# VectorE's work at three stage boundaries of a two-block network is cut into pieces and reordered

## The reference, cut to what matters

```python
# end of block 1: feed-forward, 5632 hidden columns, then gate and residual
ffn = (silu(h2 @ w_ffn_gate) * (h2 @ w_ffn_up)) @ w_ffn_down
x = x + gate2 * ffn
# block 2, layer 0: the context and the tokens are normed, modulated and projected
h_ctx = layer_norm(ctx) * (1 + sc_c) + sh_c
h_lat = layer_norm(x) * (1 + sc_l) + sh_l
z_ctx = h_ctx @ w_in_attn        # only the columns of keys and values
z_lat = h_lat @ w_in_attn
# block 2, layer 1: 4096 columns u and 4096 columns gate
u, gate = split(h @ w_in_fourier, 2)
f = fft2(u.reshape(b, l, 16, 256), axes=(1, 3), norm="ortho").real
x = post_norm(x, (f * silu(gate)) @ w_out_fourier, ...)
```

## Time and profile before

| | |
|---|---|
| three runs | 2520.95, 2525.25, 2533.34 us |
| profiled execution | 2525.53 us, span of the trace 2523.7 us |
| TensorE matmul busy | 2404.8 us, 95% of the span |
| VectorE busy | 1651.3 us, 65% |
| ScalarE busy | 1047.6 us, 42% |
| GpSimd busy | 220.7 us, 9% |
| DMA | 589.44 MB, mean 234 GB/s |
| mean granted TensorE clock | 0.981 |

### The profile page before, as it was taken

One profiled execution on the slowest core, in us unless ns is written; L12 is line 12 of the kernel. 1 busy time (PEld: TensorE's weight loads), 2 busy tenths in 40 slices (PEclk: granted clock), 3 DMA queues, 4 the chain that ended last, 5 costly groups with the idle time before them and its releaser, 6 DMA issues.

```text
span 2523.7 us, 37893 instructions
## 1 busy us (share of the span) xinstructions
PE 2404.8 (95%) x15430; PEld 2058.3 (82%) x15430; DVE 1651.3 (65%) x1869; ACT 1047.6 (42%) x1386; POOL 220.7 (9%) x200
## 2 busy tenths in 40 slices
PE   5899989989999999999999999999978999999996
PEld 1588765569888899888887888888768999999995
DVE  8655645456888888886677566555664585765557
ACT  2354764224333333333343454444443343334332
POOL 0139700011000000000011100000012000000000
PEclk9899999999999999999999999999999999999998
DMA  9844469968999999997553754334445675675451
GB/s 386 321 156 153 156 257 372 402 221 297 356 357 350 358 379 354 347 348 272 155 185 116 227 170 129 103 103 134 168 133 176 217 263 173 231 243 178 152 191 57
DMA packets 257582, 589.44 MB, mean 234 GB/s; under 512 B 20608, under 2 KB 29824, under 8 KB 256128
## 3 DMA queue, kind: packets, MB, share of 16 engines
q1 hardware_dynamic: 257408, 587.02, 67.0%
HBM read 584.85 MB, written 2.10 MB: 233 GB/s over the span
## 4 chain that ended last, share of the span: by engine, by line
PE 88%; DVE 5%; DMA 3%; ACT 2%; issue 1%; POOL 1%; SPq 0%; DVEq 0%; ACTq 0%
PE psum L213 13%; PE psum L225 13%; PE psum L227 12%; PE psum L226 12%; PE psum L215 12%; PE psum L214 12%; PE psum L297 3%; DMA start_slots<-in_w_ada 2%; DVE wlo L202 1%; PE psum L1905 1%; PE psum L2526 1%; PE psum L487 1%; PE psum L755 1%; PE psum L1919 1%; PE psum L882 1%
## 5 line engine op out<-in xcount | busy, mean ns | idle before, releaser
L202 DVE TENSOR_TENSOR wlo<-raw,whi 128x1024 fp32r<-128x1024 f32 (+2 forms) x728 | 879.6, 1224 | 558.3 <-ACT whi L196 554.9
L196 ACT CAST whi<-raw 128x1024 fp32r<-128x1024 f32 (+2 forms) x728 | 740.1, 1026 | 938.1 <-PE psum L227 491.7
L225 PE MATMUL psum<-hh,whi 128*128 128x256 f32 x2688 | 759.9, 283 | 4.9 <-DVE wlo L202 4.4
L226 PE MATMUL psum<-hh,wlo 128*128 128x256 f32 x2688 | 750.8, 279 | 0.0
L227 PE MATMUL psum<-hl,whi 128*128 128x256 f32 x2688 | 750.7, 279 | 0.0
L225 PEld LDWEIGHTS psum<-hh,whi 128*128 128x128 f32 x2688 | 507.5, 189 | 21.9 <-DVE wlo L202 11.7
L227 PEld LDWEIGHTS psum<-hl,whi 128*128 128x128 f32 x2688 | 511.5, 190 | 0.0
L226 PEld LDWEIGHTS psum<-hh,wlo 128*128 128x128 f32 x2688 | 507.8, 189 | 1.8 <-issue 1.0
L213 PE MATMUL psum<-whi,hh 128*128 128x512 f32 (+1 forms) x720 | 292.6, 406 | 9.6 <-DVE wlo L202 6.2
L215 PE MATMUL psum<-whi,hl 128*128 128x512 f32 (+1 forms) x720 | 282.3, 392 | 0.0
L214 PE MATMUL psum<-wlo,hh 128*128 128x512 f32 (+1 forms) x720 | 280.8, 390 | 0.0
(11 more groups left out here) (392 smaller groups left out, 2409.7 us busy)
## 6 DMA issues: line engine op xcount, KB each, us to landing
araw<-in_ada_w SPq DMA_DIRECT2D x128, 512.0 KB, 6.5
raw<-in_w_in_fourier SPq DMA_DIRECT2D x128, 512.0 KB, 4.1
raw<-in_w_ffn_gate SPq DMA_DIRECT2D x88, 512.0 KB, 8.8
raw<-in_w_ffn_up SPq DMA_DIRECT2D x88, 512.0 KB, 7.8
raw<-in_w_ffn_down SPq DMA_DIRECT2D x88, 512.0 KB, 9.9
raw<-in_w_in_attn SPq DMA_DIRECT2D x88, 512.0 KB, 4.5
araw<-in_w_ada SPq DMA_DIRECT2D x80, 512.0 KB, 7.1
start_slots<-in_w_ada SPq DMA_DIRECT2D x64, 512.0 KB, 8.4
```

The lines of the kernel that those rows point to most:

```text
L196: nc.scalar.copy(whi[:, u % SPLITS, 0:kn, 0:w], raw[:, u % RING, 0:kn, 0:w]).then_inc(s_hi, 1)
L202: nc.vector.tensor_tensor(wlo[:, u % SPLITS, 0:kn, 0:w], raw[:, u % RING, 0:kn, 0:w], whi[:, u % SPLITS, 0:kn, 0:w].bitcast(F32), ALU.subt ...
L225: nc.tensor.matmul(o, h, hh[:, kt + k], start=(kt + k == 0 and f % 2 == 0), stop=False)
L226: nc.tensor.matmul(o, lw, hh[:, kt + k], start=False, stop=False)
```

## The change: what is put where

1. In chunk 9 the statistics of the context stand before units 12 and 14, the moments (`ctx_moments_dve`) before unit 16, and the scalings in three pieces before units 18, 20 and 22.
2. `tail_dve` becomes three functions. The additions of the down pieces out of PSUM stand before k = -3, -1, 1, 3 and release the bank themselves; gate product and addition to x follow one unit later (k = -2, 0, 2, 4); the statistics of all four pieces come before k = 5 and 6; the norm of x before k = 7 instead of 4. The addition of piece 3 of the chunk before stands behind two low parts. The eight turns stand two units later on TensorE, VectorE and ScalarE.
3. TensorE's first Fourier product of chunk 0 stands behind unit 0 of chunk 1, and ScalarE's store of it behind the cast of unit 2 of chunk 1. VectorE's copy of u stays where it was.

```diff
@@ hidden_act
+            if H.fourier and c == 1 and j == 2:
+                hidden_store_act(act, H, 0)
...
-        if H.fourier and first:
-            hidden_store_act(act, H, c)
@@ hidden_dve
-                    if j in (18, 19):
-                        ctx_stats_dve(dve, chd[0], j - 18)
-                    if j == 21:
-                        ctx_norm_dve(dve, chd[0])
+                    if j in (12, 14):
+                        ctx_stats_dve(dve, chd[0], j // 2 - 6)
+                    if j == 16:
+                        ctx_moments_dve(dve, chd[0])
+                    if j in (18, 20, 22):
+                        ctx_norm_dve(dve, j // 2 - 9)
@@ hidden_pe
+                if H.fourier and c == 1 and j == 0:
+                    hidden_dft1_pe(pe, H, 0)
...
-        if H.fourier and first:
-            hidden_dft1_pe(pe, H, c)
@@ ctx_norm_dve in two functions
+    def ctx_moments_dve(dve, ch):
         ch(nc.vector.tensor_scalar(mscalex[:], modx[:, 16:32], 1.0, None, ALU.add))
...
+        nc.vector.tensor_scalar(ms[:], mv[:, :, 1:2], LN_EPS, None, ALU.add).then_inc(s_st, 1)
+    def ctx_norm_dve(dve, part):
+        if part == 0:
+            dve.wait_ge(s_rs, 3)
+        for t in range(TT) if part == 0 else (part - 1,):
+            cs = slice(0, CW) if part == 0 else slice(CW, D)
...
+        if part != 1:
+            ins.then_inc(s_xn, 1)
@@ ctx_pe, ctx_act
-            if 8 <= k < 16:
-                turn_pe(pe, 3, xn, 3, k - 8, k - 7)
+            if 10 <= k < 18:
+                turn_pe(pe, 3, xn, 3, k - 10, k - 9)
-            if 12 <= k < 20:
+            if 14 <= k < 22:
@@ tail_dve in three functions
+    def tail_add_dve(dve, n):
+        o = xacc[:, :, n * CW:(n + 1) * CW]
+        dve.wait_ge(s_mm, U_CTX - 6 + 2 * n)
+        nc.vector.tensor_tensor(o, o, psum[:, BANK[n]:BANK[n] + 2], ALU.add).then_inc(ffn.dv, 1)
+    def tail_gate_dve(dve, ch, n):
...
         dve.wait_ge(ffn.dv, 4 * FFN_CH - 3 + n)
+        ch(nc.vector.tensor_tensor(o, o, row2[:, cs].unsqueeze(1).broadcast_to([P, TT, CW]), ALU.mult))
+        ch.wait()
         ch(nc.vector.tensor_tensor(x[:, :, cs], x[:, :, cs], o, ALU.add))
+    def tail_stats_dve(dve, ch, n):
         for t in range(TT):
+            ch(nc.vector.bn_stats(stat[:, t, n], x[:, t, n * CW:(n + 1) * CW]))
@@ ctx_dve
-        for n in (2, 3):
-            hidden_add_dve(dve, ffn, c - 1, n)
+        hidden_add_dve(dve, ffn, c - 1, 2)
...
+            if k == -6:
+                hidden_add_dve(dve, ffn, c - 1, 3)
             if k in (-3, -1, 1, 3):
-                tail_dve(dve, ch, (k + 3) // 2)
-            if k == 4:
+                tail_add_dve(dve, (k + 3) // 2)
+            if k in (-2, 0, 2, 4):
+                tail_gate_dve(dve, ch, (k + 2) // 2)
+            if k in (5, 6):
+                if k == 5:
+                    ch.wait()
+                for n in range(2 * k - 10, 2 * k - 8):
+                    tail_stats_dve(dve, ch, n)
+            if k == 7:
...
-            if 11 <= k < 19:
-                turn_dve(dve, 3, h32, mscale, modc[:, 96:112], k - 11, k - 10)
+            if 13 <= k < 21:
+                turn_dve(dve, 3, h32, mscale, modc[:, 96:112], k - 13, k - 12)
```

More of the change, by code:

```diff
@@ L2078, in ctx_stats_dve @@
             ch(nc.vector.bn_stats(stat[:, t, c], actx[:, t, c * CW:(c + 1) * CW]))
-    def ctx_norm_dve(dve, ch):
+    def ctx_moments_dve(dve, ch):
         ch(nc.vector.tensor_scalar(mscalex[:], modx[:, 16:32], 1.0, None, ALU.add))
-        norm_rest_dve(dve, ch, 2, actx, actx, False)
+        ch.wait()
+        for t in range(TT):
+            ch(nc.vector.bn_aggr(mv[:, t], stat[:, t].rearrange("p c s -> p (c s)")))
+        ch.wait()
[5 more added lines that the diff above has]
+            cs = slice(0, CW) if part == 0 else slice(CW, D)
+            ins = nc.vector.tensor_scalar(actx[:, t, cs], actx[:, t, cs], mv[:, t, 0:1], rstd[:, t],
+                                          ALU.subtract, ALU.mult)
+        if part != 1:
+            ins.then_inc(s_xn, 1)
     def ctx_turn_pe(pe, r):
@@ L2136, in ctx_act @@
                 ctx_evac(act, k // UPC - 1)
-            if 12 <= k < 20:
-                turn_act(act, 3, h32, hh, k - 12, k - 11)
+            if 14 <= k < 22:
+                turn_act(act, 3, h32, hh, k - 14, k - 13)
             high(act, U_CTX + k, CTX[k // UPC][1])
-    def tail_dve(dve, ch, n):
+    def tail_add_dve(dve, n):
[3 more added lines that the diff above has]
+    def tail_gate_dve(dve, ch, n):
         cs = slice(n * CW, (n + 1) * CW)
         o = xacc[:, :, cs]
-        dve.wait_ge(s_mm, U_CTX - 6 + 2 * n)
-        ch(nc.vector.tensor_tensor(o, o, psum[:, BANK[n]:BANK[n] + 2], ALU.add))
+        dve.wait_ge(ffn.dv, 4 * FFN_CH - 3 + n)
+        ch(nc.vector.tensor_tensor(o, o, row2[:, cs].unsqueeze(1).broadcast_to([P, TT, CW]), ALU.mult))
         ch.wait()
-        nc.vector.tensor_tensor(o, o, row2[:, cs].unsqueeze(1).broadcast_to([P, TT, CW]), ALU.mult).then_inc(ffn.dv, 1)
-        dve.wait_ge(ffn.dv, 4 * FFN_CH - 3 + n)
         ch(nc.vector.tensor_tensor(x[:, :, cs], x[:, :, cs], o, ALU.add))
-        ch.wait()
+    def tail_stats_dve(dve, ch, n):
         for t in range(TT):
-            ch(nc.vector.bn_stats(stat[:, t, n], x[:, t, cs]))
+            ch(nc.vector.bn_stats(stat[:, t, n], x[:, t, n * CW:(n + 1) * CW]))
     def ctx_dve(dve, ch):
         c = FFN_CH
-        for n in (2, 3):
-            hidden_add_dve(dve, ffn, c - 1, n)
+        hidden_add_dve(dve, ffn, c - 1, 2)
         for k in range(-8, 3 * UPC):
```

## The result

Four runs of the changed kernel took 2504.36 to 2507.11 us, median 2505.89; the kernel before 2525.97 in the same comparison (four runs). The ratio is 0.9919, 95% interval [0.9906, 0.9932]: 0.8% faster. The interval is a gain of 17 to 24 us; the forecast was a gain of 18.2, to 2507, range 2500 to 2517. The profiled execution took 2505.13 us with a span of 2503.3, 20.4 us shorter than the span before.

The account below looks back on a forecast made before the run. TensorE was taken as the bound (88% of what ended last), so removed waits and slow clock count fully. 2.2 + 12.1 - 0.2 + 4.1 = 18.2 us off 2525.5 gave 2507; sum's range 2503 to 2511, 8-in-10 range 2500 to 2517.

Parts of the forecast that it names:

- Part 1: Context norm in chunk 9: TensorE's 2.18 us wait for down piece 0 goes; gain 2.2 us, between 0 and 2.3.
- Part 2: End of the feed-forward: chunk 10's end to context unit 7's end takes 44.2 us instead of 56.3; gain 12.1 us.
- VectorE owes 40.4 of 40.8 us: End of the feed-forward: VectorE's steps through low part 7 total 40.4 us; TensorE wants unit 7 at 40.8.
- Part 3: Turns, context unit 7 to the first token unit: 33.5 us instead of 33.3; cost 0.2, between -1.5 and +2.0.
- Part 4: First Fourier product: one 2.5 us wait before unit 0 of chunk 1, none before the product; gain 4.1 us.
- the 1.7 us of slow clock: Fourier layer: charged behind the 2.5 us wait before unit 0 of chunk 1; gain 5.8 us if the clock holds.
- VectorE as the bound of units 4 to 7: Rival, end of the feed-forward: VectorE slips 2 to 4 us, costing 4 to 7; 2511 to 2514 us; chance 0.15.
- Gain taken back: Rival, later stages: something thought TensorE bound has its own floor, such as attention weight loads; 2519 to 2526 us; chance 0.08.
- The stage at 1.2 GHz: Rival, end of the feed-forward: short waits keep the clock low through 16 wide units, up to 2549 us; chance 0.04.
- Its low end, 2503: Whole kernel: fast end of the sum's range, given as 12.8 in part 2 and the clock holding in part 4.

Follow-up runs that it names:

- e5_stats2: Changed kernel with eight more VectorE statistics instructions, into an unread buffer, beside those at context units 5 and 6; 2509.02 us (one run).
- e4_add3: Kernel before with one edit: the addition of down piece 3 of chunk 10 stands behind two low parts; 2513.93 us (one run).
- e10_poolset: Changed kernel with GpSimd's eight low parts of the turned x only writing zeros instead of reading and subtracting; 2504.59 us (one run).
- e8_turns3: Changed kernel with the norm of x before unit 8 instead of 7 and the eight turns three units earlier; 2504.74 us (one run).
- e12_tails: Changed kernel with the old undivided tails put back, keeping the later norm, the moved piece 3 addition and the later turns; 2502.78 us (one run).
- e6_copy: Changed kernel with VectorE's copy of u behind the low part of unit 0 of chunk 1 instead of ahead; 2499.1 us (one run).
- e1_norm: Kernel before with only the context norm in pieces in chunk 9; 2522.57 us (one run).
- e3_fourier: Kernel before with only the first Fourier product and its store moved; median 2520.2 us, ratio 0.9979.

## Why the prediction was right, point by point

- **Part 1, 2.2 us.** Measured 2.4, alone and in the whole. The addition was ready over 1 us early as written (1.8), and the statistics and moments cost nothing where they now stand; the other 0.2 is the restart behind the wait, which the forecast left out.
- **Part 2, 12.1 us.** Measured 11.8. The steps of VectorE's list that are read above came within 0.1 us. The wait before unit 7 was 0.68 instead of 0.6, and the end of unit 7 came 0.3 us later than forecast. What carried the result was to write both engines' queues down with prices from rows, and not the gap list alone: the gaps before are 8.1 us, the gain 11.8.
- **The statement that VectorE owes 40.4 of 40.8 us** was right for the changed kernel (e5_stats2), but used in the wrong way in e4_add3: a chain that starts at an event of TensorE moves with TensorE.
- **Part 3, -0.2 us.** Measured -0.2, with three waits as expected (0.39, 0.45 and 0.80 us in place of 0.98). e10_poolset shows that GpSimd's subtractions stand behind most of it.
- **Part 4, 4.1 us.** The wait of 2.5 us was right, 2.54. The term that was mis-sized is the 1.7 us of slow clock that I charged: in the profiled execution the clock held, which I had priced at 5.8 (measured 5.7). In four of the seven profiles with this wait it fell, and D was then 10.6, as charged (10.7). Which of the two a profile shows is luck.
- **Rivals.** VectorE as the bound of units 4 to 7: one wait only. Gain taken back: the stretches behind are the same to 0.4 us. The stage at 1.2 GHz: clock 1.00 throughout. None came.
- **The range of the sum.** Its low end, 2503, does not follow from the two terms named for it: 12.8 in part 2 and a clock that holds in part 4 give 20.6 us and 2504.9; it takes the best case of part 3 as well.
- **The total.** The forecast of 18.2 us lies within the interval of 17 to 24. That the median came out within about 1 us of 2507 is in part luck: the four runs spread over 2.8 us, and six later ones of the same kernel over 7.
- The rest of the 20.4 us, 1.1 us before chunk 9, is no effect of the change. Between two runs with 7.8 us of difference ahead of chunk 9 (e8_turns3, then e12_tails) the first 200 us look like this:

```profile
0.00:200.00 200.00, 160.63 (x933) 108.76 (x934) 132.90 (x199) 73.52 (x122) 44.14 (x45) 0.91 0.77 285
```

```profile
0.00:200.00 200.00, 163.16 (x951) 109.67 (x952) 132.86 (x199) 75.86 (x125) 47.28 (x48) 0.96 0.77 285
```

In these 200 us the spread begins, but the mean clock does not tell how it comes out. The same copy of ScalarE (L827) starts at 170.83 in e8_turns3 and at 167.51 in e12_tails, 3.3 us of the 7.8; yet in e6_copy it starts at 167.34 with a clock of 0.92, and in the kernel before at 171.16 with 0.95. The whole 7.8 us are there by the first SiLU of the feed-forward (583.81 and 576.06). From there to chunk 9's fourth copy twelve of the thirteen profiles take 651.4 us; e5_stats2 takes 646.8, and why is open, so its total is not to be compared with the others.

## What to carry to other kernels

Where one engine is the bound and another feeds it within a few units of lead, list the feeder's instructions with prices from the trace from the first event that it waits for, beside the times at which the bound engine wants each; here the one wait came out to a tenth of a microsecond. Put an instruction that releases a bank, and low parts that are ready, ahead of everything that merely has to be done sometime; then move single items until no wait is left, since a stage at 99% of the feeder has no room for more. Judge small edits by stretches between common events, not by totals.

## What the runs showed of the hardware that was not expected

- Whether the clock falls behind a wait of about 2.6 us varies between executions with the same instructions. The clearest place is one that no edit comes near, in the first block: TensorE waits 2.57 to 2.63 us for a low part at 282 to 287 us in all thirteen profiles. The clock fell directly behind it in seven and held in six. First the kernel before, where it fell, then the changed kernel, where it held:

```profile
285.52 0.80 PE L213 MATMUL psum<-whi,hh 128*128 128x512 f32 x1 [2.57 <-DVE wlo L202]
```

```profile
286.00:288.00 2.00, 2.00 (x6) 1.52 (x6) 1.55 (x2) 2.00 (x3) 1.92 (x2) 0.50 0.64 184
```

```profile
282.37 0.50 PE L213 MATMUL psum<-whi,hh 128*128 128x512 f32 x1 [2.61 <-DVE wlo L202]
...
287.17 0.50 PE L213 MATMUL psum<-whi,hh 128*128 128x512 f32 x1 [1.77 <-DVE wlo L202]
```

```profile
283.00:285.00 2.00, 2.00 (x10) 1.64 (x9) 1.77 (x2) 2.00 (x4) 1.92 (x2) 1.00 0.74 223
288.00:290.00 2.00, 2.00 (x6) 1.57 (x5) 2.00 (x2) 0.00 (x0) 1.92 (x2) 0.51 0.80 252
```

- The length of the wait alone does not decide. In all six profiles in which the clock held there, it fell behind the next wait, of 1.76 to 1.78 us, as the last rows show. Behind 2.90 us at 343 to 348 us it fell in eleven of thirteen profiles. At the Fourier layer it fell behind the 2.54 us in four of seven, at 1.6 us each (9.0 against 10.6). Behind the 2.54 us at the end of the feed-forward it fell in all three profiles that have this wait; behind 2.58 to 2.62 us before context unit 4 in three (before, e1_norm, e3_fourier), and it held in one (e4_add3). Behind the waits of 1.45 to 1.50 us in that stage and the 2.18 us in chunk 9 no profile shows a fall, and behind the 4.43 us all four that have this wait do.
- A fall can cost nothing. In the kernel before, where the clock fell at 285.52, the next matmul behind a wait starts at 290.32, 4.80 us later, after a wait of 0.31 us. In the changed kernel, where it held at 282.37, it starts at 287.17, also 4.80 us later, after 1.77 us: VectorE sets the time there.
- A wait of TensorE costs 0.3 to 0.4 us beyond its idle time at full clock: 9.1 - 6.2 - 2.54 = 0.3 us in D (changed kernel against e6_copy), 0.4 us each for the two of 1.48 us in e12_tails (B 47.4 against 43.6 in e8_turns3, which has no wait there). The first matmul takes 0.50 us instead of 0.39; the rest of the difference is not taken apart here.
